# Leaving out the identity matmuls that TensorE runs between its waits, in a trunk of mixer, router and 32 experts

## The reference, cut to what matters

```python
# x: (1, 256, 1024); all in float32
proj = x @ w_in                                   # 1024 -> 5 x 512 columns: c_b, c_c, c_h, r_x, r_g
y_conv = c_b * causal_conv(c_c * c_h, conv_w)
u = causal_conv(r_x, lru_conv_w) + lru_conv_b
y_lru = rg_lru(u, ...) * gelu(r_g)                # gates, linear recurrence over the 256 tokens
mixed = concat(y_conv, y_lru) @ w_out
x = layer_norm(alpha * x + mixed, ln1_g, ln1_b)

logits = x @ w_router + b_router                  # 32 experts
top_v, top_e = top_k(logits, 4); gates = softmax(top_v)
# per expert e, for the tokens that chose it:
h = xb @ w_gu[e] + b_gu[e]                        # 1024 -> 2048
act = min(h_glu, 7) * sigmoid(1.702 * min(h_glu, 7)) * (clip(h_lin, -7, 7) + 1)
y = act @ w_dn[e] + b_dn[e]                       # 1024 -> 1024
x = layer_norm(alpha * x + sum(gates * y), ln2_g, ln2_b)
```

## Time and profile before

| | before |
|---|---|
| median of 3 runs | 1034.14 us |
| the profiled execution | 1034.0 us |
| its span, first to last instruction | 1032.2 us |
| mean granted clock of PE | 0.938 |
| PE busy | 824.0 us (80%) |
| DVE busy | 242.0 us (23%) |
| ACT busy | 72.4 us (7%) |
| read from HBM | 421.30 MB, 409 GB/s over the span |

### The profile page before, as it was taken

One profiled execution on the slowest core, in us unless ns is written; L12 is line 12 of the kernel. 1 busy time (PEld: TensorE's weight loads), 2 busy tenths in 40 slices (PEclk: granted clock), 3 DMA queues, 4 the chain that ended last, 5 costly groups with the idle time before them and its releaser, 6 DMA issues.

```text
span 1032.2 us, 20063 instructions
## 1 busy us (share of the span) xinstructions
PE 824.0 (80%) x8413; PEld 359.0 (35%) x8414; DVE 242.0 (23%) x666; ACT 72.4 (7%) x171; POOL 6.1 (1%) x23
## 2 busy tenths in 40 slices
PE   9999879898659999986599976666966877966864
PEld 8885534333213443332133422111321322321321
DVE  2651712222111222221112211111111211211114
ACT  1300100000000000000000000000000000000000
POOL 1000000000000000000000000000000000000000
PEclk9999989999899999998899999888988998988987
DMA  9988599999999999999999999999999999999995
GB/s 337 416 323 324 212 430 425 426 422 423 429 429 428 429 428 427 429 428 429 429 429 427 429 429 429 429 427 427 428 430 429 429 427 428 429 429 429 427 427 215
DMA packets 38697, 422.62 MB, mean 409 GB/s; under 512 B 5868, under 2 KB 6296, under 8 KB 14232
## 3 DMA queue, kind: packets, MB, share of 16 engines
q1 hardware_dynamic: 36320, 421.93, 97.0%
q10 hardware_dynamic: 2360, 0.43, 0.2%
HBM read 421.30 MB, written 1.05 MB: 409 GB/s over the span
## 4 chain that ended last, share of the span: by engine, by line
DMA 49%; PE 42%; DVE 6%; issue 2%; SPq 0%; ACT 0%; DVEq 0%; POOL 0%; POOLq 0%
DMA dn_buf<-in_w_down_dram 49%; PE ps L825 16%; PE ps L853 13%; PE ps L678 5%; PE ps L721 3%; PE ps L819 2%; DVE act_t L642 1%; PE ps L695 1%; DVE lin L640 1%; DVE lin L637 1%; DVE glu L634 1%; DVE lin L635 1%; PE ps L708 0%; PE ps L740 0%; PE ps L665 0%
## 5 line engine op out<-in xcount | busy, mean ns | idle before, releaser
L825 PE MATMUL ps<-gu_buf,rows_t 128*32 128x512 f32 x2944 | 374.3, 653 | 115.3 <-DMA gu_buf<-in_w_gate_up_dram 115.3
L825 PEld LDWEIGHTS ps<-gu_buf,rows_t 128*32 128x32 f32 x2944 | 96.1, 116 | 383.3 <-issue 204.7
L853 PE MATMUL ps<-dn_buf,act_t 128*32 128x256 f32 x2912 | 174.7, 386 | 51.3 <-DMA dn_buf<-in_w_down_dram 42.9
L634 DVE TENSOR_SCALAR glu<-ps 128x256 f32<-128x256 f32 x46 | 19.5, 425 | 637.0 <-PE ps L825 637.0
L853 PEld LDWEIGHTS ps<-dn_buf,act_t 128*32 128x32 f32 x2912 | 90.3, 111 | 123.1 <-DMA dn_buf<-in_w_down_dram 55.9
L819 PE MATMUL ps<-turned,bias_sel 128*32 128x512 f32 x368 | 52.3, 641 | 23.7 <-issue 23.7
L396 ACT ACTIVATE sig<-glu 128x256 f32<-128x256 f32 x46 | 19.1, 416 | 557.1 <-DVE glu L634 557.1
L678 PE MATMUL ps<-turned,gu_buf 128*128 128x256 f32 x256 | 55.6, 379 | 0.0
L795 PE MATMUL ps<-mix,back 32*128 32x256 f32 x736 | 52.7, 400 | 0.5 <-ACT mix L400 0.5
L783 PE MATMUL ps<-xs,onehot 128*32 128x256 f32 x752 | 51.6, 393 | 0.0
L678 PEld LDWEIGHTS ps<-turned,gu_buf 128*128 128x128 f32 x256 | 48.6, 190 | 6.6
(11 more groups left out here) (164 smaller groups left out, 262.1 us busy)
## 6 DMA issues: line engine op xcount, KB each, us to landing
gu_buf<-in_w_gate_up_dram SPq DMA_DIRECT2D x128, 2048.0 KB, 28.8
dn_buf<-in_w_down_dram SPq DMA_DIRECT2D x63, 2048.0 KB, 14.5
gu_buf<-in_w_in_dram SPq DMA_DIRECT2D x4, 2048.0 KB, 18.2
gu_buf<-in_w_out_dram SPq DMA_DIRECT2D x2, 2048.0 KB, 14.8
xs<-in_x_dram SPq DMA_DIRECT2D x2, 512.0 KB, 3.8
gu_buf<-in_w_in_dram SPq DMA_DIRECT2D x2, 512.0 KB, 6.2
gu_buf<-in_w_in_dram SPq DMA_DIRECT2D x1, 1024.0 KB, 8.9
late<-in_ln_g_dram SPq DMA_DIRECT2D x2, 512.0 KB, 24.1
```

The source lines that it names most:

```text
L634: V.tensor_scalar(glu[:], half(HB, 0), SWIGLU_LIMIT, None, ALU.min).then_inc(S["glu_ok"], 1)
L825: ins = T.matmul(ps[SLOTS * j:SLOTS * (j + 1), HB, :], rows_t[:, k, :], gu_buf[:, b, k, :].rearrange("p (two n) -> p two n", two=2)[:, :, ...
L853: ins = T.matmul(ps[SLOTS * j:SLOTS * (j + 1), YB, 0:QF], act_t[:, DK * m + q, :], weights[q][:, QF * j:QF * (j + 1)], start=(m == 0 and q ...
```

## The change

Every call of `keep_warm` goes, and the function with it: 27 matmuls, 7 before the first projection and 20 in and around the router. Nothing is moved, and no wait, DMA or operation of another engine changes.

```diff
-            def keep_warm(bank, n):
-
-                for _ in range(n):
-                    T.matmul(ps[:, bank, 0:P], ident[:], ident[:], start=True, stop=True)
-            keep_warm(TB, 5)
             for h in range(TH):
                 pe.wait_ge(S[f"x_in{h}"], 16)
...
-            keep_warm(TB, 2)
             project_first((4, 5))
...
             for h in range(TH):
                 for c in range(2):
-                    if h and c == 0:
-                        keep_warm(Y0, 5)
                     pe.wait_ge(S["x1_ok"], 2 * h + c + 1)
...
                 else:
-                    keep_warm(Y0, 3)
                     pe.wait_ge(S["x1t_act"], 3)
...
             ins.then_inc(S["lpart_ps"], 1)
-            keep_warm(Y1, 1)
             pe.wait_ge(S["lpart_sb"], 1)
...
             ins.then_inc(S["logits_ps"], 1)
-            keep_warm(Y1, 6)
...
-            keep_warm(Y1, 4)
             pe.wait_ge(S["onehot0"], 1)
             gather().then_inc(S["rows0_ps"], 1)
...
             pe.wait_ge(S["bgu_in"], 16 * GROUPS)
-            keep_warm(HB, 1)
```

## The result

The changed kernel takes 1037.62 us in the median of 20 runs (1036.19 to 1041.43); the kernel before, run beside it, 1035.16 us (1033.02 to 1037.30). The medians lie 2.5 us apart; the ratio, for which there is an interval, is 1.0027 (95% interval 1.0019 to 1.0035): 2.8 us slower, between 2.0 and 3.6. The forecast was 3.1 us more. The profiled execution of the changed kernel took 1038.35 us, its span 1036.6 us, 4.4 us more than that of before.

The account below looks back on a forecast made before the run. PE's way to the weight stream's restart at 125.6 us, then full-rate DMA, bound the kernel. Launch +0.6, queue -0.3 and clock +2.8 gave +3.1 us on 1034.14, so 1037.2 us; range for all cases 1034.0 to 1039.5.

Parts of the forecast that it names:

- The frame: Time is PE's finish of the first expert block's first chunk, plus an unchanged weight stream, plus tail; delays pass on fully.
- Part 1: Launch, before the first projections: PE starts later, its clock rises later, early projections run at half pace; +0.6 us.
- and so the start stays at 7.6 us: Launch: slower transposes are offset by two later identity matmuls going, so the first projection still starts at 7.6 us.
- the same 4.7 us after the first matmul: Launch: the clock rises 4.7 us after PE's start at 4.16, at 8.9 us, so 0.65 us is lost.
- Part 2: Router, PE's queue: only the last identity matmul, before the first block's bias matmuls, occupies time; removing it gains 0.32 us.
- Part 3: Router, PE's clock: it falls between some 113 and 118 us and slows the critical steps behind; +2.8 us, bounds 1.2 to 4.1.
- the partial logits: Router, L762, 16 records in four rounds: at the lower clock they cost +0.45 us.
- from there to the first expert matmul: Router, gather, transpose and bias matmuls at the lower clock: first expert matmul +0.8 us later, +1.1 against the queue gain.
- the first chunk: First expert block's first 16 records: the clock rises at 126.5 to 127.0 us, about 1.3 us at half pace, +0.65 us.
- A: Rival, router: short bursts keep the clock up, so 1034.4 us, or 1033.5 if the launch gains too; chance 0.18.
- B: Rival, launch: transposes don't count as work for the clock, the rise comes at about 12.3 us, 1038.9 us; chance 0.11.
- C: Rival, whole path: DMA or ACT ends the waits, so the delay is swallowed and time is 1034.5 us; chance 0.06.

Follow-up runs that it names:

- the run of the launch alone: Kernel before without only the seven identity matmuls of the launch, the router's twenty kept: ratio 0.9998 (0.9989 to 1.0007), -0.2 us.
- the router's own run: Also called the router alone: kernel before without only the twenty identity matmuls in and around the router, the launch's seven kept: ratio 1.0024, 2.5 us slower.
- the transposes: Kernel before with every identity matmul issued as transposes of the identity, twice as many: ratio 0.9996 (0.9987 to 1.0004).
- the run with ten more: Kernel before with fourteen identity matmuls instead of four ahead of the first gather: ratio 1.0013 (1.0002 to 1.0024), 1.3 us slower.
- the early nine: Kernel before without the nine identity matmuls before and between the router's transposes and partial logits, later eleven kept: ratio 1.0014, 1.5 us slower.

## Why the prediction was right, and where its steps were off

**The frame held.** The last down matmuls follow the first L261 issue at a fixed distance, within 1.7 us, and the dependence on PE's way there is one to one as far as the traces can tell. The tail behind them scatters more than I had said: from the first L261 issue to the end of the span are 905.9 to 906.6 us in the four traces with the router's twenty in place (in one of them as transposes), 906.3 to 907.6 in the four without them. That doesn't show that the change lengthens the tail: with only the last of the twenty out it is 907.7 us.

**Part 1, the launch, was mis-sized: +0.6 predicted, -0.2 (-1.1 to +0.7) measured.** The mechanism is there: half pace between the first projection and the rise, 0.64 us in one trace and 1.9 us in the profiled one. What failed is the step "and so the start stays at 7.6 us". I took 7.60 us for a start that PE's queue sets, as it did in the trace of before. In most traces it is set by the landing of the first piece of `w_in`: PE waits for it in five of the eight traces with the launch's matmuls in, which start at 7.47 to 8.33 us, and in three of the four without them, which start at 8.20 to 8.49. With a start near 8.2 us a rise at 7 or 7.4 us costs nothing, and one at 9.2 us half a microsecond. The other step, a rise "the same 4.7 us after the first matmul", held in one trace of four: with the first transpose at 4.15 to 4.32 us the four rises came about 3, 3, 5 and 8 us behind it. The 12.3 us of the profiled execution is the exception, and 1.9 of its 4.4 us come from it. Anyone who explained the result from that trace alone would have given the launch over half of the effect; the run of the launch alone takes that back.

**Part 2, the queue: -0.32 predicted, -0.21 measured.** The place was right. I had counted the whole interval between two starts as free, and about 0.1 us of it stayed.

**Part 3, the clock: +2.8 predicted; with part 2 +2.5, measured 1.7 to 2.1 in the traces and 2.5 (1.6 to 3.4) in the times.** Step by step in the profiled execution, each counted from the first router transpose: the second L752 +0 (0.2 predicted; the clock fell after it, as in all four traces), the partial logits +0.44 (0.45), L768 +0.43 (0.3), the bf16 matmuls +0.01 (0.1), from there to the first expert matmul +1.09 (0.8, which is 1.1 less the 0.3 of part 2), the first chunk 0 (0.65). The last is the term that made the sum too large: I let the clock rise at 126.5 to 127.0 us, after the chunk had begun at 125.4, and in three of the four traces it rose as the chunk began, some 4 us behind the start of the gather (124.38 us in the profiled one) and not 5; in the fourth it rose within the bias matmuls.

Both errors go the same way: with -0.2 for the launch and 2.0 for the router the sum would be 1.8 us, under the 2.8 (2.0 to 3.6) that was measured, as the router's own run gave 2.5 by its times and 1.9 by its trace. Each of the numbers from the times has an interval of nearly 1 us to either side, so the gap isn't shown to be real; whether the tail holds a part of it isn't shown either. The closeness of 1037.2 to 1037.62 is in part luck: I had added 3.1 us to a median of 1034.14, and the kernel before took 1035.16 beside the changed one. On that the same forecast would have been 1038.3 us.

**The rivals.** A fell with the router alone, B with the transposes, C with the constant distance, though not by the times alone. What I named for A, that long pauses precede the falls, wasn't answered by the two falls that I had dated: the 2.27 us of the earlier trace rows belong to a pause of 2.95 us in one piece. But the same trace has as long a pause with the clock at 1.00 for the 5 us behind it. Timeline of PE, then windows of all engines, of before:

```profile
193.07 2.60 PE L853 MATMUL ps<-dn_buf,act_t 128*32 128x256 f32 x32 [2.95 <-DMA dn_buf<-in_w_down_dram]
...
663.37 1.93 PE L853 MATMUL ps<-dn_buf,act_t 128*32 128x256 f32 x32 [2.97 <-DMA dn_buf<-in_w_down_dram]
...
661.80:665.20 3.40, 1.83 (x32) 0.94 (x32) 0.00 (x0) 0.00 (x0) 0.00 (x0) 1.00 0.97 414
665.20:668.60 3.40, 1.51 (x16) 0.32 (x16) 0.00 (x0) 0.37 (x1) 0.00 (x0) 1.00 1.03 439
```

And the longest pause before the fall in the changed kernel is 1.68 us, shorter than the 2.2 us I had named. So neither is a long pause needed, nor was one enough.

**Open.** Why the rise came so late in the profiled execution (12.3 us, with PE at work from 4.32 us but for 0.52 us) and near 7 and 7.4 us in two others isn't settled; four traces only show that it varies. It does so with the seven matmuls in as well: the 16 transposes of x took 2.53 us in one of those eight traces and 3.67 in another, where 3.65 us is the lower pace throughout. How the launch's cost averages out below 0.7 us was not resolved either.

## What to carry to other kernels

Matmuls that fill waits are worth their place where PE's short bursts stand on the path and nothing hides them: twenty of them, in a router of 17 us, hold 2.5 us of a kernel of 1035 us that is bound by DMA otherwise. At the launch look first for what the first real matmul waits for; where that is a DMA, a slower PE ahead of it is hidden. And look at where the clock falls before you take out some of the fillers: once it has fallen, the rest of them run at half pace and can end behind the event that they were to bridge. With the early nine out the eleven that stayed delayed the gather in this way, and that trace's router was no shorter than without any; by the times (1.5 and 2.5 us, with overlapping intervals) it isn't shown which of the two is worse.

## What the runs showed of the hardware

- Transposes of float32, 128 columns each, raise and hold the clock as matmuls do (projections at full pace from 7.41 us after nothing but transposes; with transposes as fillers 1.00 through the router).
- The clock fell though no pause of PE was longer than 1.68 us, after 2.9 us of work in 5.4 to 5.9 us of short bursts, and then stayed at 0.50 for ten microseconds; so in the three traces whose windows stand above. A pause of 2.97 us in the trace of before was followed by 5 us at 1.00.
- The first piece of `w_in`, issued at the same time in each execution, lands at a different time in each: in the eight traces in which PE waited for it, the first projection started at 7.47 to 8.49 us.
- The tail has its own share in the scatter: the last 32 down records took 1.93 or 1.94 us in eight of the traces, but 2.43 to 3.27 us in four, of kernels that don't differ there. What makes them longer wasn't looked into. The row of the run with ten more:

```profile
1018.86 3.27 PE L853 MATMUL ps<-dn_buf,act_t 128*32 128x256 f32 x32 [2.83 <-DMA dn_buf<-in_w_down_dram]
```
